# First norm by pairs of token tiles and x turned in 16 units, in a one-core decoder-layer kernel

## The reference

```python
cond = jax.nn.silu(c)
ada = cond @ w_ada[l] + b_ada[l]                      # 1024 x 6144
shift1, scale1, gate1, shift2, scale2, gate2 = split(ada, 6)
h = rms_norm(x) * (1.0 + scale1) + shift1
proj = h @ w_in[l]           # q_a, k_a, v_a | q_g, k_g, v_g, g_out, z_lr
attn = sliding_window_attention(...)                  # 8 heads, window 128
gla = ...                                             # 4 heads, chunks of 64
x = x + gate1 * (concat(attn, gla) @ w_out[l])
h = rms_norm(x) * (1.0 + scale2) + shift2
x = x + gate2 * (square(relu(h @ w_mlp_in[l])) @ w_mlp_out[l])
return rms_norm(x) * final_norm_g
```

## Time and profile before

| | us |
|---|---|
| Median of 3 runs | 1026.87 (1026.24 to 1026.91) |
| Time of the profiled execution | 1026.08 |
| Its span in the trace | 1024.3 |
| TensorE busy | 1006.9 (98% of the span) |
| VectorE busy | 692.1 (68%) |
| ScalarE busy | 463.3 (45%) |
| GpSimd busy | 76.8 (7%) |

### The profile page before, as it was taken

The page is one execution under the profiler, slowest core; times in us unless marked ns, Lnnn a source line. Parts: engine busy times, 40 slices in busy tenths (PEclk is TensorE's granted clock), DMA queues, the critical chain, the costliest instruction groups (busy, mean ns, idle before and its releaser), DMA issues.

```text
span 1024.3 us, 12728 instructions
## 1 busy us (share of the span) xinstructions
PE 1006.9 (98%) x4947; PEld 809.5 (79%) x4947; DVE 692.1 (68%) x911; ACT 463.3 (45%) x763; POOL 76.8 (7%) x114
## 2 busy tenths in 40 slices
PE   6999999999999999999999999999999999999997
PEld 5677778877777888888888888888888888888885
DVE  4677578688884547986655655654559955388886
ACT  7420012377773016856455455456344344344443
POOL 0122100011111000000000000001231000101100
PEclk9999999999999999999999999999999999999999
DMA  9987633300014424254533533249996322545624
GB/s 333 319 234 261 228 124 104 83 1 2 1 43 177 111 83 165 83 198 172 184 142 126 185 144 123 103 153 327 347 386 204 123 83 103 206 163 186 212 95 164
DMA packets 94643, 165.93 MB, mean 162 GB/s; under 512 B 15579, under 2 KB 44924, under 8 KB 94460
## 3 DMA queue, kind: packets, MB, share of 16 engines
q1 hardware_dynamic: 82700, 122.61, 35.5%
q0 software_dynamic: 11888, 42.55, 11.6%
HBM read 127.37 MB, written 39.34 MB: 163 GB/s over the span
## 4 chain that ended last, share of the span: by engine, by line
PE 95%; DMA 2%; DVE 1%; ACT 1%; SPq 1%; issue 0%; DVEq 0%; ACTq 0%
PE bank L1248 23%; PE bank L1198 19%; PE bank L953 13%; PE score_banks L1198 7%; PE score_banks L1248 6%; PE score_banks L724 4%; PE bank L724 4%; PE score_banks L953 4%; PE bank L1209 2%; PE bank L990 2%; PE score_banks L1012 1%; DMA ada_chunk<-in_w_ada 1%; PE score_banks L849 1%; PE score_banks L1209 1%; PE bank L849 1%; PE bank L1067 1%
## 5 line engine op out<-in xcount | busy, mean ns | idle before, releaser
L1248 PE MATMUL bank<-dn_hi,hid_hi 128*128 128x512 f32 x352 | 136.9, 389 | 0.0
L1248 PE MATMUL bank<-dn_lo,hid_hi 128*128 128x512 f32 x352 | 136.9, 389 | 0.0
L1248 PE MATMUL bank<-dn_hi,hid_lo 128*128 128x512 f32 x352 | 136.9, 389 | 0.0
L2382 ACT ACTIVATE hid_hi<-hid_raw 128x1024 fp32r<-128x1024 f32 x56 | 58.9, 1051 | 151.8 <-PE bank L1248 151.8
L1858 DVE TENSOR_TENSOR hid_lo<-hid_raw,hid_hi 128x1024 fp32r<-128x1024 f32 x56 | 68.3, 1220 | 83.4 <-ACT hid_hi L2382 83.4
L1725 DVE TENSOR_TENSOR up_lo<-up_raw,up_hi 128x1024 fp32r<-128x1024 f32 x48 | 58.7, 1223 | 58.6 <-ACT up_hi L2275 58.6
L2275 ACT ACTIVATE up_hi<-up_raw 128x1024 fp32r<-128x1024 f32 x48 | 50.5, 1057 | 69.8 <-PE score_banks L1198 31.2
L2062 ACT ACTIVATE w_hi<-raw 128x2048 fp32r<-128x2048 f32 x11 | 21.1, 1915 | 129.9 <-PE bank L724 81.6
L1248 PEld LDWEIGHTS bank<-dn_hi,hid_lo 128*128 128x128 f32 x352 | 66.1, 188 | 13.8
L1248 PEld LDWEIGHTS bank<-dn_hi,hid_hi 128*128 128x128 f32 x352 | 66.1, 188 | 13.8
L1248 PEld LDWEIGHTS bank<-dn_lo,hid_hi 128*128 128x128 f32 x352 | 66.1, 188 | 13.6
(11 more groups left out here) (361 smaller groups left out, 2293.5 us busy)
## 6 DMA issues: line engine op xcount, KB each, us to landing
hidden_forms<-hid SPq DMA_DIRECT2D x56, 512.0 KB, 3.1
hid_raw<-hidden_forms SPq DMA_DIRECT2D x56, 512.0 KB, 3.8
ada_w<-in_w_ada POOLq DMA_DIRECT2D x32, 512.0 KB, 5.5
up_raw<-in_w_mlp_in SPq DMA_DIRECT2D x32, 512.0 KB, 5.2
dn_ring<-in_w_mlp_out POOLq DMA_DIRECT2D x24, 512.0 KB, 6.0
raw<-in_w_in SPq DMA_DIRECT2D x34, 256.0 KB, 4.2
ada_chunk<-in_w_ada SPq DMA_DIRECT2D x16, 512.0 KB, 9.6
dn_t<-in_w_mlp_out POOLq DMA_DIRECT2D x16, 512.0 KB, 8.4
```

The lines of the kernel that those rows point to most:

```text
L1248: mm = pe.matmul(b, (hid_hi, hid_lo)[x][n % 2][:, k, t * P:(t + 1) * P], (dn_hi, dn_lo)[y][n % 2][:, k, :], start=(first and i == 0), stop ...
L2382: a.activation(hid_hi[n % 2][:, ks, :], hid_raw[n % 2][:, ks, :], ACT.Copy).then_inc(s_dhi, 1)
```

## The change

The sixteen turned banks become sixteen units. Unit number 4p + q holds the two feature tiles 2q and 2q + 1 of the pair p of token tiles (2p and 2p + 1), so that a pair that is normed gives four units. `UNIT_BANK` spreads them over all eight banks, `UNIT_V` and `UNIT_S` say which engine reads which: six by VectorE, ten by ScalarE. The norm is done in four pairs in place of two halves (`pair_scaled` on VectorE, `pair_root` on ScalarE). ScalarE takes Ln from the sum of squares itself, with the division as its scale and epsilon in a column that GpSimd fills (`eps_col`), so that it does not wait for the variance; VectorE scales all eight tiles. The identity and `b_rows` are issued between the second and third tile of x. There are 20 transposes of the identity in place of 24, and the transpose of `b_rows` stands right behind them. The first half of quarter 1's sum, which stood ahead of the first slot, stands behind its products of the high part for k = 0. The semaphore counts of the second norm follow, with no change of what it does.

```diff
@@ -68,7 +68,10 @@
 COL = 32
-V_TURNED = ((0,), (0, 1, 2, 3, 4, 6))
+PAIRS = NT // 2
+UNIT_BANK = (0, 1, 2, 3, 4, 5, 6, 7, 0, 1, 2, 3, 4, 5, 7, 0)
+UNIT_V = (0, 1, 8, 10, 12, 14)
+UNIT_S = (2, 3, 6, 4, 5, 7, 9, 11, 13, 15)
 PRODUCTS = ((0, 0), (0, 1), (1, 0))
...
@@ -368,14 +371,27 @@
     BACK_FIRST = (32, 16 * (COPIES + 1))
-    SQ_FIRST = ROOT_FIRST = RMS_FIRST = 4
+    SQ_FIRST = ROOT_FIRST = RMS_FIRST = PAIRS + 2
     SCALED_FIRST = len(AFF_S)
-    def turned_ready(half, k):
-        if k in V_TURNED[half]:
-            return s_turned_v, half * len(V_TURNED[0]) + V_TURNED[half].index(k) + 1
-        return s_free, half * KT + k + 1
+    def turned_ready(unit):
+        if unit in UNIT_V:
+            return s_turned_v, UNIT_V.index(unit) + 1
+        return s_free, G_F if unit == UNIT_S[-1] else UNIT_S.index(unit) + 1
+    def pair_turned(q):
+        units = [4 * p + q for p in range(PAIRS)]
+        for of in (UNIT_V, UNIT_S):
+            mine = [u for u in of if u in units]
+            if mine:
+                yield turned_ready(mine[-1])
+    def unit_out(unit):
+        p, q = unit // 4, unit % 4
+        return (act_full[:, 2 * q:2 * q + 2, p * 256:(p + 1) * 256],
+                bank[UNIT_BANK[unit]][:, :].rearrange("p (k t) -> p k t", k=2))
@@ -444,19 +460,19 @@
             for t in range(NT):
-                if t == 4:
+                if t == 2:
                     sp.dma_start(ident[:, :], identity).then_inc(s_ident, 16)
+                    sp.dma_start(b_rows, b_ada[0].rearrange("(k p) -> k p", p=P)).then_inc(s_b_rows, 16)
                 sp.dma_start(x_in[:, t, :], x_d[:, t, :]).then_inc(s_x[t], 16)
-            sp.dma_start(b_rows, b_ada[0].rearrange("(k p) -> k p", p=P)).then_inc(s_b_rows, 16)
             ada_first(0)
...
             ada_first(1)
-            sp.wait_ge(s_nrm[0], 1)
+            sp.wait_ge(s_nrm[0], 2)
             ada_first(2)
...
                 sp.dma_start(raw_k(0)[:, 2 * j:2 * j + 2, :], w_in_d[:, 2 * j:2 * j + 2, QG0:QG0 + 256]).then_inc(s_rest, 16)
-            sp.wait_ge(s_nrm[1], 2)
+            sp.wait_ge(s_nrm[0], PAIRS)
             ada_first(3)
...
@@ -783,18 +800,21 @@
-            def turn_half(half, ks):
-                pe.wait_ge(s_nrm[half], half + 1)
-                for k in ks:
-                    g = half * KT + k
-                    if g >= 4:
-                        h, j = (g - 4) // KT, (g - 4) % KT
-                        pe.wait_ge(*turned_ready(h, j))
-                    for t in range(4):
-                        mm = pe.transpose(bank[g % 4][:, t * P:(t + 1) * P],
-                                          x_nrm[:, 4 * half + t, k * P:(k + 1) * P], ident[:, :])
-                    mm.then_inc(s_full, 1)
+            def turn_unit(unit):
+                p, q = unit // 4, unit % 4
+                if q == 0:
+                    pe.wait_ge(s_nrm[0], p + 1)
+                if UNIT_BANK[unit] in UNIT_BANK[:unit]:
+                    pe.wait_ge(*turned_ready(max(u for u in range(unit) if UNIT_BANK[u] == UNIT_BANK[unit])))
+                for k in range(2):
+                    for t in range(2):
+                        mm = pe.transpose(bank[UNIT_BANK[unit]][:, (2 * k + t) * P:(2 * k + t + 1) * P],
+                                          x_nrm[:, 2 * p + t, (2 * q + k) * P:(2 * q + k + 1) * P], ident[:, :])
+                mm.then_inc(s_full, 1)
+            def bank_read(b):
+                pe.wait_ge(*turned_ready(max(u for u in range(16) if UNIT_BANK[u] == b)))
@@ -831,7 +851,7 @@
                     if k == 0 and 0 in products:
-                        pe.wait_ge(*turned_ready(1, 4 + 2 * half + m))
+                        bank_read(2 * half + m)
                     for n in products:
@@ -852,20 +872,26 @@
             pe.wait_ge(s_ident, 16)
-            for i in range(24):
+            for i in range(20):
                 pe.transpose(bank[7][:, i % 4 * P:(i % 4 + 1) * P], ident[:, :], ident[:, :])
-            turn_half(0, range(7))
-            pe.wait_ge(s_set, 4)
-            chunk_sum(0, 0)
-            turn_half(0, (7,))
             pe.wait_ge(s_b_rows, 16)
             pe.transpose(bank[5][:, 0:6 * KT], b_rows, ident[0:6 * KT, 0:6 * KT]).then_inc(s_b_full, 1)
-            turn_half(1, (0,))
+            for unit in range(4):
+                turn_unit(unit)
+            pe.wait_ge(s_b_col, 1)
+            for unit in range(4, 12):
+                turn_unit(unit)
+            pe.wait_ge(s_set, 4)
+            bank_read(6)
+            chunk_sum(0, 0)
+            turn_unit(12)
             chunk_sum(0, 1)
-            turn_half(1, (1, 2))
+            turn_unit(13)
+            turn_unit(14)
+            bank_read(4)
             chunk_columns(0)
-            turn_half(1, range(3, KT))
-            chunk_sum(1, 0)
+            turn_unit(15)
             def high_act(k, half):
@@ -877,6 +903,9 @@
                         first_slot(k, half, (n,))
+                if k == 0:
+                    bank_read(7)
+                    chunk_sum(1, 0)
             chunk_sum(1, 1)
...
@@ -1367,19 +1396,24 @@
-            def norm_scale(half, tiles):
-                norm_newton(half, 0)
-                v.wait_ge(s_rms, half + 1)
-                for t in tiles:
+            def pair_scaled(p):
+                cols = slice(2 * p, 2 * p + 2)
+                v.wait_ge(s_sq, p + 1)
+                v.tensor_scalar(var[:, cols], ssq[:, cols], 1.0 / D, EPS, ALU.mult, ALU.add).then_inc(s_var, 1)
+                v.wait_ge(s_var, p + 1)
+                v.wait_ge(s_root, p + 1)
+                newton(rstd[:, cols], var[:, cols], newt[:, cols]).then_inc(s_rms, 1)
+                v.wait_ge(s_rms, p + 1)
+                for t in (2 * p, 2 * p + 1):
                     ins = v.tensor_scalar(x_nrm[:, t, :], x_in[:, t, :], rstd[:, t:t + 1], None, ALU.mult)
-                ins.then_inc(s_nrm[half], 1)
-            def turned_out(half, k):
-                full(half * KT + k)
-                v.tensor_copy(act_full[:, k, half * HALF:(half + 1) * HALF], bank[(half * KT + k) % 4][:, :])\
-                    .then_inc(s_turned_v, 1)
+                ins.then_inc(s_nrm[0], 1)
+            def turned_out(unit):
+                dst, src = unit_out(unit)
+                full(unit)
+                v.tensor_copy(dst, src).then_inc(s_turned_v, 1)
@@ -1404,8 +1438,8 @@
                 v.wait_ge(s_ada_col, k // 2 + 1)
-                v.wait_ge(*turned_ready(0, k))
-                v.wait_ge(*turned_ready(1, k))
+                for ready in pair_turned(k // 2):
+                    v.wait_ge(*ready)
                 own.link(v.tensor_scalar(act_aff[:, k, :], act_full[:, k, :], ada_col[:, KT + k:KT + k + 1],
@@ -1420,22 +1454,19 @@
             v.tensor_copy(cond_pad[:, :, 0:1], cond.unsqueeze(2)).then_inc(s_set, 1)
-            norm_var(0, 0)
-            norm_scale(0, range(4))
-            norm_var(1, 0)
-            turned_out(0, 0)
-            norm_scale(1, range(4, NT - 1))
+            pair_scaled(0)
             v.wait_ge(s_b_full, 1)
...
             v.tensor_scalar(b_col[:, KT:2 * KT], b_col[:, KT:2 * KT], 1.0, None, ALU.add).then_inc(s_b_col, 1)
-            turned_out(1, 0)
-            turned_out(1, 1)
-            turned_out(1, 2)
+            pair_scaled(1)
+            turned_out(0)
+            pair_scaled(2)
+            turned_out(1)
+            pair_scaled(3)
+            for unit in UNIT_V[2:]:
+                turned_out(unit)
             v.wait_ge(s_b_col, 1)
             first_columns(0)
-            turned_out(1, 3)
-            turned_out(1, 4)
-            turned_out(1, 6)
             first_half_lo()
...
@@ -2069,7 +2100,7 @@
                 ins = a.activation(dst[:, t, :], src[:, t, :], ACT.Square, accum_out=ssq[:, t:t + 1])
-                if t % 4 == 3:
+                if t % 2 == 1:
                     ins.then_inc(s_sq, 1)
@@ -2077,17 +2108,24 @@
-            def turned_out(half, k):
-                a.wait_ge(s_full, half * KT + k + 1)
-                a.activation(act_full[:, k, half * HALF:(half + 1) * HALF], bank[(half * KT + k) % 4][:, :], ACT.Copy)\
-                    .then_inc(s_free, {(0, 1): 2, (1, 5): 6, (1, 7): 2}.get((half, k), 1))
+            def turned_out(unit):
+                dst, src = unit_out(unit)
+                a.wait_ge(s_full, unit + 1)
+                a.activation(dst, src, ACT.Copy).then_inc(s_free, G_F - len(UNIT_S) + 1 if unit == UNIT_S[-1] else 1)
+            def pair_root(p):
+                cols = slice(2 * p, 2 * p + 2)
+                a.wait_ge(s_sq, p + 1)
+                own.link(a.activation(lnv[:, cols], ssq[:, cols], ACT.Ln, scale=1.0 / D, bias=eps_col))
+                a.activation(rstd[:, cols], lnv[:, cols], ACT.Exp, scale=-0.5).then_inc(s_root, 1)
...
                 a.wait_ge(s_ada_col, k // 2 + 1)
-                a.wait_ge(*turned_ready(0, k))
-                a.wait_ge(*turned_ready(1, k))
+                for ready in pair_turned(k // 2):
```

(34 more changed lines are left out.)

6 lines of the change are left out of this document (3 added, 3 removed).

## The result

| | before | changed |
|---|---|---|
| Median of the runs compared | 1026.41 (1026.00 to 1026.91, 5 runs) | 1031.45 (1030.80 to 1031.67, 5 runs) |
| Profiled execution | 1026.08 | 1031.45 |
| Its span | 1024.3 | 1029.7 |

What follows compares the result with a forecast made beforehand. TensorE, busy 98% of the span, was taken as the bound after a DMA landing at 20.43 us. A first slot 1.07 later plus 1.19 for the moved half sum made 2.26 us, put on the 1026.87 median: 1029.1, range 1027.0 to 1030.8.

Steps and rivals of the forecast that it cites:

- The order of ScalarE: Before the first slot: copies of units 13 and 15 precede the sum's copy and the cast; first slot 1.07 us later.
- the moved half sum: Between products after the first slot's start: 0.99 us plus 0.20 for refilling the pipe, 1.19 in all, with nothing covering it.
- the landing: Arrival of the second half of quarter 0 of `w_ada`, at 20.43 us: unchanged, plus or minus 0.3.
- the clock: TensorE's granted clock around the idle time before the first slot: stays at full, PEclk 1.00 throughout, costing nothing.
- Up to the landing: From the start to 20.43 us: the first transpose's head start of 3.3 us is spent in waiting; second half sum unchanged.
- VectorE's 0.94 us of waiting for the bias: After pair 0, before 11.1 us: VectorE idles 0.9 us for the bias's transpose, with pair 1 behind it.
- ScalarE never late: During the norm: ScalarE has the last root ready at 16.1 us and isn't what pair 3 waits for.
- unit 12: Ahead of the second half sum on TensorE: done at about 20.4 us, with 0.1 us to spare.
- The chain: From the second half sum at 20.48 us to the first slot at 27.18: 1.07 us later than before.
- Rival B: Before the first slot: idling halves TensorE's clock, costing 2.6 us more, 4.9 in all, 1031.8 us; chance 0.10.
- The forecast's own range: For the whole kernel, from uncertain copy costs, pipe fill and DMA arrival: 1.5 to 2.9 us, 1028.4 to 1029.8.
- The range: For the whole kernel's time: 1027.0 to 1030.8 us, holding the forecast and leaving out a fallen clock.

Runs made afterwards that it cites:

- kernel 3: The kernel before, with only the load of `b_rows` moved early, between the second and third tile of x: 1026.69 us against 1026.21.
- kernel 4: The changed kernel, with `b_rows` issued behind the fourth tile of x and the identity left early: 1030.39 us against 1026.21 for the kernel before.
- Kernel 7: The changed kernel, with ScalarE copying quarter 0's sum ahead of unit 13 and casting the first weights ahead of unit 15's copy: 1028.03 us.
- kernel 5: The changed kernel, with 24 more identity transposes, result not read, between the last unit of x and the first slot: 1029.75 us.
- kernel 6: The changed kernel, with the first half of quarter 1's sum put back ahead of the first slot: 1028.59 us.
- kernel 2: The kernel before, with only the identity issued early, between the second and third tile of x: 1028.29 us against 1026.16.
- kernel 9: The changed kernel, with identity and `b_rows` issued behind the fourth tile of x, `b_rows` turned first, and 2 identity transposes for 20: 1031.11 us.
- kernel 1: The kernel before, with the identity and `b_rows` both issued between the second and third tile of x: 1029.26 us against 1026.03.
- kernels 8: The changed kernel, with identity and `b_rows` issued behind the fourth tile of x and `b_rows` turned ahead of the identity transposes: 1031.22 us.

## Why the prediction was wrong

The sign was right and the size was not: 5.0 us where 2.26 were forecast. The order of ScalarE and the moved half sum, from which the 2.26 was made, cost within 0.2 us what they were said to cost. What failed are the two terms that the sum put at nothing: the landing, which was to stay and came 1.1 later, and the clock, which was to hold and cost some 1.6. By its own steps:

- **Up to the landing.** VectorE's 0.94 us of waiting for the bias and ScalarE never late came as forecast. The step that failed is "The bytes ahead of that transfer are the same, so the landing stays", plus or minus 0.3. The bytes were the same, the rate was not: 298 GB/s between 6 and 8 us for 412, and the landing 1.1 later, 0.9 if counted from the first tile's. In the medians the effect of `b_rows` is 0.5 (kernel 3) and 0.9 (kernel 4 against the changed one). That unit 12 was out of the way in time was luck in part: it was to be done at about 20.4, and began at 20.46, behind pairs that came 0.3 to 0.5 late, so that it would have stood in the way of a landing at 20.43. In kernel 4 the half quarter landed at 20.32 and TensorE was busy with unit 12 until 20.51.
- **After the landing, ScalarE's order.** Measured from the sum's start, the copy of unit 13 came 1.69 later (forecast 1.68), the sum's copy 2.18 (2.17), the cast 4.57 (4.45), `act_hi` 5.52 (5.40), the first slot 6.89 (6.70). The chain costs 1.26 in place of 1.07; 0.09 of the difference is `chunk_columns`, which also waits for VectorE's copy of unit 14. I had left that out; the wait ahead of it was forecast (22.35 to 23.31) and is the 0.8 of L834 among the waits, but VectorE's copy ended it, and not the sum's. Kernel 7 confirms the cause.
- **The moved half sum**, 1.19, was right: 1.22 between kernels 5 and 6. Together with the clock kernel 6 gives 2.5 (by the differences from before) to 2.9 (between the medians), where 1.2 and 1.56 make 2.8.
- **The clock.** The forecast held it at full, and that failed; the rival that said otherwise had the mechanism right and its chance too low. Rival B had 0.10 and "half of the 5.2 us that the start needed", 2.6. It happened, and cost 1.56 by the chain and 1.3 to 1.7 by kernel 5. I had argued from the end of the kernel, where 3.8 idle microseconds passed before the clock fell. That one row was read as a bound, and it isn't one: the clock fell after 2.91 us here and after 2.60 in kernel 2, in kernels 9 and 1 it fell when TensorE had been idle for 1.5 and 2.1 us, and in kernel 7 it held through 2.03. What the prediction took from the Trainium skill (TensorE: Matmul & The Clock Gate, Part 1: The HAM clock gate), that idling brings the half clock back, was the better guide here.
- **The sum.** 1.1 + 1.26 + 1.2 + 1.56 = 5.1, and at the group that started at 40.78 it was 5.13. The remaining 0.3 of the span's 5.4 came later; a wait that is longer by 0.1 (the 0.5 of L1227, before 0.4) lies there, and I can't name the rest.

If the landing and the clock are taken out, 1.26 + 1.2 = 2.46 remains, against the forecast's 2.26. The forecast's own range is added up slightly wrong: its deductions, twice 0.19, the 0.20 and the 0.3, take 2.26 down to 1.4 and not to 1.5. The range had no room for two of its side cases at once, though they were not exclusive: a later landing and a fallen clock add to each other.

## What to carry to other kernels

Moving a small load forward can move more than its bytes: look at the data rate where it will stand and at the landing of the last large transfer behind it. Where an engine waits for a DMA, work that is brought forward is spent in the wait unless the chain behind the landing gets shorter too; look there for what the change puts ahead of the critical copy on every engine. And count a TensorE wait like the ones of 2.60 and 2.91 us here as a chance, not a remote one, to lose its clock: put useful work into it, and take none out.

## What the runs showed of the hardware

- The clock's fall after an idle stretch is not fixed by its length: after 2.91 idle microseconds it fell about 0.95 us after work had resumed (changed kernel), 0.5 and 0.4 after it (kernels 8 and 4), or 1.4 before it (kernel 9), so 1.5 us into the idle stretch. It held through the 2.03 of kernel 7. It stayed at half for 3.4 us in the changed kernel and for about 6.8 in kernel 9.
- Work done to raise the clock too early is lost: in kernel 1 the last transposes of the identity stepped at 0.11 us, the full clock, and after 5.09 idle microseconds TensorE was at half; in kernel 2 it still was at full when it went on after 2.60 idle microseconds, and fell 0.87 us later. There the first slot came 1.5 us later than before, 0.36 of them for another reason.
- Sixteen DMA engines can be listed as busy (1.00 and 0.92 between 6 and 8 us in the changed kernel and kernel 3) while they move 298 and 342 GB/s in place of 412: their busy share doesn't show such a gap, the rate does.
